# Twelve heads for the taps, 34 rows left for the mixer and a packed decode in a two-block kernel

## The reference, cut to what matters

```python
hx = modulate(x, sh1, s1)
q, k, v, u = split_cols(hx @ w_in[l])
o_attn = attend_latent(q, k_all, v_all)             # 8 heads, 512 keys
o_conv = conformer_conv(u, conv_w[l], ...)          # 31 taps, layer norm, silu
x = x + g1 * merge_groups(o_attn, o_conv, beta_attn[l], beta_conv[l], w_o[l])
x = x + g2 * peer(modulate(x, sh2, s2), peer_wq[l], peer_keys[l], peer_u[l], peer_v[l])
# peer: per token 8 heads x 16 best of 16384 experts ("picks"); u and v rows of each pick are
#   i1 = take(top_i[..., 0, :], best_j // 16); i2 = take(top_i[..., 1, :], best_j % 16)
#   act = gelu(h . u_row);  out = sum over the picks of act * weight * v_row
```

## Time and profile before

| what | value |
|---|---|
| median of 3 runs | 3023.49 us (3018.86 to 3025.12) |
| the profiled execution, its own time | 2998.16 us |
| its span, first to last instruction | 2996.3 us |
| busy: PE, DVE, POOL, ACT | 83%, 71%, 37%, 28% |
| DMA over the span | 1038.89 MB, mean 347 GB/s |
| granted PE clock, mean | 0.906 |

### The profile page before, as it was taken

One profiled execution on the slowest core, in us unless ns is written; L12 is line 12 of the kernel. 1 busy time (PEld: TensorE's weight loads), 2 busy tenths in 40 slices (PEclk: granted clock), 3 DMA queues, 4 the chain that ended last, 5 costly groups with the idle time before them and its releaser, 6 DMA issues.

```text
span 2996.3 us, 27808 instructions
## 1 busy us (share of the span) xinstructions
PE 2473.3 (83%) x8610; PEld 1397.2 (47%) x8610; DVE 2117.1 (71%) x4458; ACT 831.8 (28%) x2284; POOL 1113.1 (37%) x1121
## 2 busy tenths in 40 slices
PE   6995888888898989888788787778888887787776
PEld 4653464666455666565444333323464444333322
DVE  1659579788879878786687677754374776777654
ACT  1231111000102000114444343344224443433343
POOL 1100445666554665360233333333210333343332
PEclk9987887999896999987999899899988999899999
DMA  8358999999999999860699999999821999999998
GB/s 343 152 185 335 378 412 363 397 406 412 391 411 358 403 406 412 339 253 1 246 405 408 369 420 419 416 414 393 330 73 39 364 417 369 420 420 419 415 420 335
DMA packets 183478, 1038.89 MB, mean 347 GB/s; under 512 B 26971, under 2 KB 28978, under 8 KB 99876
## 3 DMA queue, kind: packets, MB, share of 16 engines
q0 software_dynamic: 147456, 805.37, 66.6%
q1 hardware_dynamic: 35292, 230.38, 19.3%
q10 hardware_dynamic: 584, 1.36, 0.1%
HBM read 1032.60 MB, written 4.44 MB: 346 GB/s over the span
## 4 chain that ended last, share of the span: by engine, by line
PE 31%; DMA 29%; DVE 25%; issue 7%; POOL 4%; ACT 4%; SPq 0%; ACTq 0%; DVEq 0%; POOLq 0%
DMA W<-in_peer_uv,IDX 14%; PE PS L2659 12%; PE PS L323 11%; DMA ROWS<-in_peer_uv,IDX 5%; DVE ROWS L1345 4%; DMA ROWS<-in_peer_uv,COEF 3%; POOL ROWS L2490 3%; DVE W L2790 2%; DMA ROWS<-in_peer_uv,IDXV 2%; DVE ROWS L2284 2%; PE PS L2085 2%; DMA G<-in_peer_uv,IDX 1%; PE PS L2095 1%; PE PS L459 1%; DVE H L2297 1%
## 5 line engine op out<-in xcount | busy, mean ns | idle before, releaser
L2659 PE MATMUL PS<-W,SCALE 128*128 128x512 f32 x1712 | 834.2, 633 | 223.0 <-ACT SCALE L2743 222.7
L2790 DVE CUSTOM_DVE_ANT_0 W<-W,PS 128x1024 f32<-128x1024 f32 x428 | 515.4, 1220 | 332.3 <-DMA W<-in_peer_uv,IDX 331.2
L2843 POOL DMA_INDIRECT W<-in_peer_uv,IDX x428 | 407.0, 951 | 683.2 <-PE PS L2659 665.1
L2659 PEld LDWEIGHTS PS<-W,SCALE 128*128 128x128 f32 x1712 | 327.8, 201 | 708.9 <-issue 707.7
L2490 POOL DMA_INDIRECT ROWS<-in_peer_uv,IDX x206 | 213.4, 1036 | 408.1 <-DVE IDX L1606 155.3
L2085 PE MATMUL PS<-XT,W 128*128 128x256 f32 x1408 | 307.3, 379 | 0.0
L2085 PEld LDWEIGHTS PS<-XT,W 128*128 128x128 f32 x1408 | 267.8, 190 | 45.5 <-issue 10.1
L2736 ACT ACTIVATE DOT<-DOT 128x1 f32<-128x1 f32 x512 | 103.6, 202 | 657.1 <-DVE DOT L2790 650.7
L323 PE MATMUL PS<-W,XT 128*128 128x512 f32 (+2 forms) x576 | 220.0, 544 | 10.8 <-ACT XT L945 5.7
L323 PE MATMUL PS<-XT,W 128*128 128x128 f32 (+1 forms) x1344 | 215.4, 320 | 6.2 <-ACT XT L1058 6.2
L2743 ACT ACTIVATE SCALE<-C,COEF 128x128 f32<-128x128 f32 x512 | 205.6, 402 | 48.4 <-PE PS L2659 1.2
(11 more groups left out here) (397 smaller groups left out, 3173.0 us busy)
## 6 DMA issues: line engine op xcount, KB each, us to landing
W<-in_w_up SPq DMA_DIRECT2D x44, 1024.0 KB, 12.0
W<-in_w_in SPq DMA_DIRECT2D x21, 2048.0 KB, 11.5
W<-in_w_mod SPq DMA_DIRECT2D x7, 4096.0 KB, 12.9
W<-in_w_down SPq DMA_DIRECT2D x22, 1024.0 KB, 8.0
W<-in_peer_wq SPq DMA_DIRECT2D x6, 2048.0 KB, 11.2
W<-in_w_o SPq DMA_DIRECT2D x6, 2048.0 KB, 9.8
W<-in_w_out SPq DMA_DIRECT2D x4, 2048.0 KB, 12.4
W<-in_peer_uv,IDX POOLq DMA_INDIRECT x428, 12.8
```

The lines of the kernel that those rows point to most:

```text
L2659: ins = nc.tensor.matmul(PS[:, SUMS2[t] + h, :], SCALE[:, n % NSCALE, :], v_of(n)[:, h * 512:(h + 1) * 512], start=m == 0, stop=m == PICKS ...
L2790: nc.vector.tensor_tensor_reduce(u_of(n), u_of(n), h_of(t), 1.0, 0.0, ALU.mult, ALU.add, DOT[:, t, m:m + 1]).then_inc(s.rows_used, 1)
L2843: nc.gpsimd.indirect_dma_start(pair_slot(n), None, in_pairs, bass.IndirectOffsetOnAxis(IDX[:, t, m:m + 1], 0),).then_inc(pair_landed[fetch ...
```

## The change

- **Taps.** In both latent mixers the 31 taps are spread over heads 0 to 11 (`taps_at`: two or three behind each). What followed is written in another order: the attention branch of half 0 is turned at once, keys are turned early, heads 13 and 14 stand between the products, and before `turn_h(0)` all heads but 15 are through. The context's mixer stays.
- **Left rows.** `LEFT` is 34. Eight fewer rows are summed beside the first block's second layer. 18 (`LEFT_EARLY`) are summed where the 26 were; 16 (`LEFT_LATE`) inside the mixer of latent layer 0, fetched through four places (`LATE_SLOTS`) once PE has turned the conv, and added by DVE to `FG`. Key scores of head 0 are copied only when all 34 are in. SP stores `FG` instead of `H`, behind the layer's weight loads.
- **Packed decode**, context only: three indices of the 16 are packed into one number, so that the one-hot has 6 places instead of 16, and a shift and a mask take the index out again.

```diff
+TAP_HEADS = 12
+def taps_at(i):
+    return range(TAPS2 * i // TAP_HEADS, TAPS2 * (i + 1) // TAP_HEADS)
+
-LEFT = 26
+LEFT = 34
+LEFT_LATE = 16
+LEFT_EARLY = LEFT - LEFT_LATE
+LATE_SLOTS = 4
...
-            SUMS = [[15] * 8, [13] * 3 + [12] * 5]
+            SUMS = [[15] * 8, [12] * 3 + [11] * 5]
...
+def left_sums(dve, i0, i1):
+    for i in range(i0, i1):
+        m = PICKS - LEFT + i
+        left_in(dve, i)
+        if i:
+            dve.wait_ge(left_used, i)
+        nc.vector.scalar_tensor_tensor(H[:, 0, :] if i < LEFT_EARLY - 1 else FG[:], ROWS[:, left_slot(i), :], COEF[:, 0, m:m + 1],
+                                       H[:, 0, :] if i < LEFT_EARLY else FG[:], ALU.mult, ALU.add).then_inc(left_used, 1)
```

POOL, behind the layer's small matrices; and SP, where the store is taken out behind the gates and put behind the weight loads:

```diff
+            if left:
+                pool.wait_ge(s.groups_done, groups.of("convT", TT - 1))
+                for i in range(LEFT_EARLY, LEFT):
+                    if i >= LEFT_EARLY + LATE_SLOTS:
+                        pool.wait_ge(left_used, i - LATE_SLOTS + 1)
+                    left_fetch(i)
...
-                if left:
-                    sp.wait_ge(left_used, LEFT)
-                    sp.dma_start(cs_dram[L - 1], H[:, 0, :]).then_inc(s.stored, 16)
...
+                    if l == 0:
+                        sp.wait_ge(left_used, LEFT)
+                        sp.dma_start(cs_dram[L - 1], FG[:]).then_inc(s.stored, 16)
```

ACT, behind the heads with taps:

```diff
+            exps(12)
+            probs_turned(10)
+            branch_turned("O", 0)
+            root(act, s, TT, 3, 1.0, 0)
...
+            exps(13)
+            probs_turned(11)
+            for t in range(TT):
+                silu(t)
+            branch_turned("Y", 0)
+            root(act, s, 2, 4, 1.0 / CW2, 1)
...
+            if left:
+                act.wait_ge(left_used, LEFT)
             scores_in(0, 0)
```

DVE, behind `y_scale_ready`; and the decode of the context's picks:

```diff
+            late_left(4)
+            maximum(14)
+            late_left(5)
+            add_product("Y", 0, 0, r[:, 1:2])
+            late_left(2)
+            add_product("Y", 0, 1, r[:, 1:2])
             dve.wait_ge(s.mix_read, 2)
             link(nc.vector.tensor_tensor(H[:, 0, :], H[:, 0, :], B["ROW"][0], ALU.mult))
             onto_x(0)
             statistic(squares(SRC[:, 0, :], 5, 0))
+            late_left(1)
             scaled_h(0, 5)
             shifted_h(0)
+            late_left(4)
...
+                link(nc.vector.scalar_tensor_tensor(word, tf[:, :, WORDS:2 * WORDS], 256.0, tf[:, :, 0:WORDS], ALU.mult, ALU.add))
...
+                    ins = nc.vector.tensor_reduce(B["EI"][:, c, picks], hot[c].rearrange("p (n b) -> p n b", b=WORDS), AX, ALU.add)
...
+                link(nc.vector.tensor_tensor(held, held, shift, ALU.logical_shift_right))
```

More of the change, by code:

```diff
@@ L54 @@
 PICKS = EH * TOPK
+WORDS = 6
 N_EXP = EK * EK
@@ L401, in left_in @@
             beside = (L * 2 * PICKS - LEFT - 1 - slot) // BESIDE + 1
-            engine.wait_ge(row_landed[slot], 16 * (beside + (1 if i < RING else 2 + (i - RING) // (RING - 2))))
+            engine.wait_ge(row_landed[slot], 16 * (beside + sum(left_slot(j) == slot for j in range(i + 1))))
         def left_fetch(i):
@@ L813, in product, with turn_keys @@
                 groups.at["product", name, t, c, "bank"] = b
[L815 to L848, removed]
+            def turn_keys(g):
                 b = banks.take(s.keysT_ready, g + 1)
@@ L854, in latent_mixer_pe @@
                 groups.at["keys", g, "bank"] = b
-            score(13)
-            turn_probs(11)
-            sum_values(10)
+            banks.leave_out(5)
+            banks.hold(5, s.conv_ready, 2)
+            for i in range(TAP_HEADS):
+                score(i)
+                taps(taps_at(i))
+                if i >= 2:
+                    turn_probs(i - 2)
+                if i >= 3:
+                    sum_values(i - 3)
+            head(12)
+            pe.wait_ge(s.conv_ready, 2)
+            banks.put_back(5)
+            for t in range(TT):
+                turn_conv(t)
+            pe.wait_ge(s.merged_ready, 1)
+            turn_branch("O", 0)
+            pe.wait_ge(s.late_rows_loaded, 16 * 2)
+            for g in range(2):
+                turn_keys(g)
+            head(13)
+            for c in range(2):
+                product("O", 0, c, s.y_read, c + 1)
+            pe.wait_ge(s.act_out_ready, 1)
+            turn_branch("Y", 0)
+            head(14)
+            for c in range(2):
+                product("Y", 0, c, s.mix_read, c + 1)
+            pe.wait_ge(s.act_out_ready, 2)
+            turn_branch("Y", 1)
+            turn_probs(13)
+            sum_values(12)
+            for c in range(2):
+                product("Y", 1, c, s.y_read, 2 + c + 1)
             for b in (2, 3):
@@ L896, in CT_tok, with stream_sp @@
             return CT[:].rearrange("p k s -> p (k s)").rearrange("p (t d) -> p t d", t=TT)
-        def stream_sp(sp, s, groups, B, l, who, beside=None, first=0, left=False, before=None):
+        def stream_sp(sp, s, groups, B, l, who, beside=None, first=0, before=None):
             m = mod_dram[l][who:who + 1]
@@ L1111, in branch_turned @@
                 ins.then_inc(s.catT_ready, 1)
-            for i in range(QH):
+            for i in range(TAP_HEADS):
                 exps(i)
@@ L1151, in latent_mixer_act @@
             probs_turned(11)
+            for t in range(TT):
+                silu(t)
+            branch_turned("Y", 0)
+            root(act, s, 2, 4, 1.0 / CW2, 1)
+            act.wait_ge(s.y_scale_ready, 1)
+            if left:
+                act.wait_ge(left_used, LEFT_EARLY)
+            for c in range(2):
+                b = bank("product", "O", 0, c)
+                nc.scalar.activation(H[:, 0, c * 512:(c + 1) * 512], PS[:, b, :], ACT.Copy, scale=ri[:, 0, 0:1]).then_inc(s.y_read, 1)
+            exps(14)
+            probs_turned(12)
+            branch_turned("Y", 1)
+            probs_turned(13)
+            root(act, s, 1, 5, 1.0 / D, 1)
+            for c in range(2):
+                b = bank("product", "Y", 1, c)
+                nc.scalar.copy(H[:, 1, c * 512:(c + 1) * 512], PS[:, b, :]).then_inc(s.y_read, 1)
             h_turned(0)
             queries_in(0, 0)
+            if left:
+                act.wait_ge(left_used, LEFT)
             scores_in(0, 0)
@@ L1199, in stream_pool @@
             if left:
-                for i in range(LEFT):
+                for i in range(LEFT_EARLY):
                     if i >= RING:
```

124 lines of the change are left out of this document (58 added, 66 removed).

## The result

| | before | changed |
|---|---|---|
| median, five runs each | 3024.58 us (3018.86 to 3028.75) | 3009.34 us (3003.80 to 3012.20) |
| the profiled execution, its own time | 2998.16 us | 3011.31 us |

A forecast was written before the change was run, and what follows sets the result against it. No engine bounds the whole, so each edit is worth what its own stage gives: 10.3 + 8 + 1 + 14.5 = 34 us off 3023.5, 2989.5 us; forecast's own range 2979 to 3002, with rivals 2976 to 3010.

The forecast's parts named there:

- 18 sums instead of 26: Latent layer 0 ahead of rot_ready: fewer early left sums let norms start sooner; 8 us gained (3 to 10), at most 10.1.
- the prediction's other working: Early left rows beside w_o loads: DMA engines alternate between queues, rows get half the bandwidth, last lands about 3 us late.
- The contended landing time: Last early left row among weight loads: median landing 14.2 us instead of 6.3; 7.9 us lost, 3.3 stay.
- The turn of the ring: Reuse of four row places; for late rows in mixer 0, sum 1.4 plus issue and landing, 8.5 us per four rows.
- Sixteen late sums: Mixer of latent layer 0: late sums leave 1 us of gain there, search about 55.5 us behind the last tap.
- there by then: Mixer 0: the first four late rows have landed when DVE may start sums at y_scale_ready, 19 us behind the last tap.
- Taps over twelve heads: Both latent mixers: last tap to search 42 us against 58.85, less 2.4 for maxima; 14.5 us gained in layer 1.
- near 1.0 as the prediction named for a sign: PE behind the mixers' last tap: granted clock near 1.0, against 0.50 in the first 20.4 us before.
- Eight rows fewer: First block, second layer, bound by DMA: eight fewer rows save 10.3 us (6 to 12), a pair takes 21.8 us.
- Packed decode: Setup, context's picks: near 5 us less for each of two searches, worth 0 because DVE waits 7.57 us for ACT.
- The base: Whole kernel: gain taken off the 3023.5 us median, 25 us above the profiled 2998.16 us; 2989.5 us.
- transfers take most of it: Rival, chance 0.22: w_o loads delay early rows, late ring takes 9 us, first block gives 7; 12 us gained, 3011.

The follow-up runs named there:

- hold_wo: Changed kernel with SP waiting for the 18 early left sums before latent layer 0's late weight loads; ratio 0.9897, 2993.05 us.
- loose26: As taps_alone, but SP starts the late weight loads without waiting for the 26 left sums and stores behind them; ratio 0.9982, 2990.03 us on another chip.
- early34: Changed kernel with all 34 left rows summed early, store and weight loads behind them, no late sums; ratio 0.9894, 3002.50 us.
- the repeats: Changed kernel run and profiled twice more without edits: 3011.22 us in one run, then ratio 0.9951, 3007.84 us on another chip.
- hold_fill: As hold_wo, with the first four late sums moved ahead of the reciprocal for y_scale; ratio 0.9866, 2988.81 us; repeated on another chip 0.9904, 2993.70 us.
- taps_alone: Kernel before with only the mixers' new order (taps over twelve heads), 26 early left rows, last sum to FG, old decode; ratio 0.9921, 2997.94 us.
- taps_second: taps_alone run again without edits, on the chip of the changed kernel's third profile; ratio 0.9915, 2998.42 us.
- before_again: Kernel before, unchanged, profiled a second time; 3027.26 us in one run.

## Why the prediction was wrong

Faster was right, the size was not: 15 us instead of 34. Step by step:

**18 sums instead of 26: forecast 8 (3 to 10), measured -1 to -2.** This step failed. 38.1 and 38.8 us to the norms before, 40.0, 41.1 and 39.2 after. The prediction saw that SP would no longer hold back the `w_o` loads, and summed what had to go through: 4 MB of loads and some 3 MB of rows, 17 us, the last row 1299 - 1271.2 = 27.8 us behind the first left sum. It landed 1323.6 - 1285.3 = 38.3 us behind it. From the first load to that row 6.29 MB of loads and 3.95 MB of rows went through, in 26.7 us.

The third 2 MB load is the first `peer_wq`, which PE's progress lets start at 1314 and which the sum left out; it came ahead of the last row, after a stretch in which the rows had only a fifth of the bytes beside `w_o`, where the prediction's other working gave them half. The contended landing time that it took for the last row, 14.2 us, was too low too: 19.9.

hold_wo puts the price at 13.8 us with 18 rows, loose26 at 17.5 with 26. At the 421 GB/s of 1302 to 1312 the loads that got in first are 6.29 MB / 421 = 15 us and 8.39 / 421 = 20 us (estimates), near enough that bytes alone can account for it. The turn of the ring is no part of it in the changed kernel, where POOL did not wait for a sum behind the ninth fetch; in loose26 it did, for another 15 us in four waits, and what that adds is not shown. With the loads held back the step is worth 12 us at the norms (38.1 to 26.2), two more than its bound of 10.1, and first left sum to first maximum goes from 58.6 to 46.0 us: 10.25 us of that is PE's wait, and the turns take 1.47 us at the full clock instead of 2.82.

**Sixteen late sums: forecast 1 gained in layer 0 with the taps, measured 4 lost.** Mixer 0 takes 107.4 to 109.0 us against 104.0 and 104.4; by early34 the sums cost 17.0 us where the forecast had 14.5 - 1 = 13.5. The mechanism was right, the term too small, within its bounds: `y_scale` at 21.8 us instead of 19, `h` at 50.2 instead of 49, the last row at 55.6 instead of 54.6, and 2.83 us from the last sum through ACT's copy to the search instead of 0.9. That is 2.9 us of the miss; the other 2.0 lie ahead of the last tap, where the heads took 49.9 us instead of 45.5 + 2.4 (47.6 and 50.2 in the repeats, 48.1 in hold_wo), with DVE waiting up to 1.04 us for PE at the first maxima. The four rows that the prediction had "there by then" lay unused while DVE stood idle for 7.89 us; hold_fill took 7 us out of that.

**Taps over twelve heads: forecast 14.5 in layer 1, measured 14.4 in the mean.** Mixer 1 went from 104.6 and 105.4 us to 91.2, 90.2 and 90.2; last tap to search 42 to 43 us, heads with taps 2.4 us longer. taps_alone and taps_second show 12 to 13 in layer 0 as well. The window behind the taps went from a clock of 0.50 to 0.74 and 0.80, not to near 1.0 as the prediction named for a sign. The products' 22.8 us (the 48 are records, 24 multiplies) measured 23.9 in layer 1 of the changed kernel.

**Eight rows fewer: forecast 10.3, measured some 9.** In the profiles with the episode, the first block takes 985 us with 26 left rows (983.5, 986.1, 989.5, 980.4) and 976 with 34 (eight, from 973.2 to 980.8); the two groups touch, so the size is good to a few us. 7.6 us of it are on PE between the first and the last `up` product of the second layer, before_again and the changed kernel:

```profile
1025.51 27.79 PE L2085 MATMUL PS<-XT,W 128*128 128x256 f32 x128
...
1248.34 13.98 PE L2085 MATMUL PS<-XT,W 128*128 128x256 f32 x64
```

```profile
1020.86 27.79 PE L2137 MATMUL PS<-XT,W 128*128 128x256 f32 x128
...
1236.09 13.98 PE L2137 MATMUL PS<-XT,W 128*128 128x256 f32 x64
```

222.8 and 215.2 us. In the changed kernel the last two steps from pair to pair are 20.7 us, PE's floor; over the last eight the mean is 22.5 us, 22.4 and 21.8 in the repeats, against 23.4 and 23.5 before, where 21.8 was forecast for 23.1.

**Packed decode: forecast 0, measured nothing that can be told from 0.** It is hidden behind ACT, as the prediction said.

**The base.** Taking the gain off the median and not off the profile was right: the profile had no episode, while runs of before take 3023 to 3030 us on the chips whose profiles have one. That it came from another chip than the timed runs is likely and not shown.

Sum by stages: 9 in the first block, - 1.6, - 4.1, 14.4, about 1 lost in the picks: 16.7 us, where 15 were measured. Of the rivals on record "transfers take most of it" came nearest (12 us, 3011 us), in part by luck: the loads that delay the early rows are its mechanism, but it still kept 3 us of that term, and it lost 10 in layer 0 to a slow ring that turned nearly as forecast. What stays open: taps_alone and taps_second spend 758.3 and 760.2 us in the picks of layer 0, before 762.7 and 764.1, loose26 762.4 and the others 763.9 to 767.5; no run tells why.

## What to carry to other kernels

A wait that looks like order alone (a store that stood ahead of loads) can be what keeps small fetches quick. When a change lifts it, count the bytes of every load that can start before the last of those fetches has landed, not only of the first ones let loose, and count them at the share that the small packets really get. Before placing work behind a semaphore, look for idle time on its engine just ahead of it: four sums behind `y_scale` cost 7 us that were free two lines earlier. And take a change apart before it is judged: its first part alone was 9.4 us faster than the whole on one chip, and on another it took 2997.94 us against 3011.22 in a single run of the whole.

## What the runs showed of the hardware

Where plain loads and indirect row fetches were both waiting, DMA took packets from the two queues in equal number: 224 and 227 in the ten us shown above for the changed kernel. The loads' packets were four times as large, so they had 3.38 MB of it and the rows 0.82.

The same kernel takes 2994.40 us on one chip and 3022.90 to 3030.38 us on three others. Most of it is one episode of some 30 us, at the same place in either kernel, in which TensorE issues single multiplies with idle times of 0.2 to 2.9 us between them (rows of before_again above) and nothing in the profile ends the wait. It lies in a stretch in which DMA is full (1.02 of its engines and 413 GB/s in the window of the changed kernel below, and the same figures in the first profile of before, without the episode); in 780 to 1000 us the profiles with it show 341 to 348 GB/s, the other two 387 and 390. Each chip was used at one time only, so chip and time can't be told apart, and what causes the episode is not settled.

```profile
844.00:876.00 32.00, 18.91 (x23) 5.63 (x22) 18.59 (x32) 1.66 (x3) 17.27 (x19) 0.63 1.02 413
```
